# Feed-forward gate and up products: seven block products per feature pair in place of eight, in float32 on one Trainium2 core

## What is computed

```python
D_FF = 2816

def _swiglu(h, w1, w3, w2):
    return (jax.nn.silu(h @ w1) * (h @ w3)) @ w2

def second_block(x, ...):
    ...
        x = x + 0.5 * _swiglu(_rms_norm(x, ffn1_norm[layer]),
                              ffn1_w1[layer], ffn1_w3[layer], ffn1_w2[layer])
        ...
        x = x + mixed @ w_out[layer]
        x = x + 0.5 * _swiglu(_rms_norm(x, ffn2_norm[layer]),
                              ffn2_w1[layer], ffn2_w3[layer], ffn2_w2[layer])
```

## Time and profile before

| | us |
|---|---|
| median of 3 runs (lowest, highest) | 2481.8 (2480.57, 2481.88) |
| span of the profiled execution | 2479.0 |
| TensorE busy | 2412.7 (97%) |
| VectorE busy | 1413.9 (57%) |
| ScalarE busy | 1041.5 (42%) |
| GpSimd busy | 288.2 (12%) |

### The profile page before, as it was taken

The page is one execution under the profiler, slowest core; times in us unless marked ns, Lnnn a source line. Parts: engine busy times, 40 slices in busy tenths (PEclk is TensorE's granted clock), DMA queues, the critical chain, the costliest instruction groups (busy, mean ns, idle before and its releaser), DMA issues.

```text
span 2479.0 us, 30754 instructions
## 1 busy us (share of the span) xinstructions
PE 2412.7 (97%) x12348; PEld 1874.9 (76%) x12348; DVE 1413.9 (57%) x2056; ACT 1041.5 (42%) x1571; POOL 288.2 (12%) x248
## 2 busy tenths in 40 slices
PE   6999999999899999999999999999999999999999
PEld 4877868687777777777666688888888777888887
DVE  3675776768645777555555674344444767543442
ACT  2424433343545456655555562222343555322221
POOL 0010111212232411111111100000122000000000
PEclk9999999999999999999999999999999999999999
DMA  7324234342446369999999722332332112323322
GB/s 278 115 67 171 90 136 132 102 132 83 141 158 228 121 256 400 424 423 423 423 422 423 313 85 86 101 102 78 101 115 71 43 43 68 103 81 107 96 78 81
DMA packets 116083, 427.77 MB, mean 173 GB/s; under 512 B 15977, under 2 KB 30569, under 8 KB 90208
## 3 DMA queue, kind: packets, MB, share of 16 engines
q1 hardware_dynamic: 91488, 377.42, 41.3%
q10 hardware_dynamic: 13440, 25.17, 2.8%
q0 software_dynamic: 11008, 23.16, 2.7%
HBM read 411.08 MB, written 31.72 MB: 179 GB/s over the span
## 4 chain that ended last, share of the span: by engine, by line
PE 77%; DMA 10%; DVE 8%; ACT 4%; issue 1%; SPq 0%; ACTq 0%; POOL 0%; DVEq 0%; POOLq 0%
PE bank L762 19%; PE bank L764 18%; PE bank L763 18%; DMA pair<-in_ed 8%; PE bank L1354 2%; PE bank L1332 1%; PE bank L1334 1%; PE bank L1333 1%; DVE HLB L432 1%; PE bank L1404 1%; DVE HLB L295 1%; ACT HLB L421 1%; PE bank L1713 1%; DMA raw<-in_wxbc 1%; PE bank L1736 1%
## 5 line engine op out<-in xcount | busy, mean ns | idle before, releaser
L432 DVE TENSOR_TENSOR HLB<-raw,HLB 128x1024 fp32r<-128x1024 f32 (+1 forms) x286 | 346.1, 1213 | 369.9 <-ACT HLB L421 369.6
L762 PE MATMUL bank<-HTh,HLB 128*128 128x512 f32 (+1 forms) x1358 | 545.2, 401 | 10.4 <-DVE HLB L432 7.5
L764 PE MATMUL bank<-HTh,HLB 128*128 128x512 f32 (+1 forms) x1358 | 528.8, 389 | 0.0
L763 PE MATMUL bank<-HTl,HLB 128*128 128x512 f32 (+1 forms) x1358 | 524.9, 387 | 0.0
L421 ACT ACTIVATE HLB<-raw 128x1024 fp32r<-128x1024 f32 (+1 forms) x294 | 289.8, 991 | 298.3 <-PE bank L764 270.9
L762 PEld LDWEIGHTS bank<-HTh,HLB 128*128 128x128 f32 x1358 | 257.1, 189 | 90.7 <-issue 27.5
L764 PEld LDWEIGHTS bank<-HTh,HLB 128*128 128x128 f32 x1358 | 256.4, 189 | 57.1
L763 PEld LDWEIGHTS bank<-HTl,HLB 128*128 128x128 f32 x1358 | 257.1, 189 | 53.0 <-issue 1.9
L763 PE MATMUL bank<-FAl,HLB 128*128 128x512 f32 x352 | 138.9, 395 | 0.0
L764 PE MATMUL bank<-FAh,HLB 128*128 128x512 f32 x352 | 138.9, 395 | 0.0
L762 PE MATMUL bank<-FAh,HLB 128*128 128x512 f32 x352 | 138.9, 395 | 0.0
(11 more groups left out here) (632 smaller groups left out, 4432.5 us busy)
## 6 DMA issues: line engine op xcount, KB each, us to landing
raw<-in_f SPq DMA_DIRECT2D x120, 512.0 KB, 3.4
pair<-in_ed SPq DMA_DIRECT2D x32, 1024.0 KB
ht_pair<-in_eu SPq DMA_DIRECT2D x31, 1024.0 KB, 22.5
raw<-in_wada SPq DMA_DIRECT2D x40, 512.0 KB, 4.1
raw<-in_eg SPq DMA_DIRECT2D x17, 1024.0 KB, 7.1
pair<-in_eu SPq DMA_DIRECT2D x17, 1024.0 KB
ht_pair<-in_eg SPq DMA_DIRECT2D x17, 1024.0 KB
ht_pair<-in_ed SPq DMA_DIRECT2D x16, 1024.0 KB, 20.0
```

The lines of the kernel that those rows point to most:

```text
L432: self.nc.vector.tensor_tensor(lo, raw, hi.bitcast(F32), ALU.subtract).then_inc(*self.w_lo.next(n))
L762: mm(bank, ah, bh, start=(start and i == 0), stop=False)
L763: mm(bank, ah, bl, start=False, stop=False)
L764: ins = mm(bank, al, bh, start=False, stop=(stop and i == n - 1))
```

## The change

Of the 11 feature pairs of a network, pair 0 stays as it was. In the ten others w1 and w3 are taken as one matrix. For a pair, the weights form 2 x 2 blocks: rows are the even and the odd feature (each with its 128 columns of w1 and of w3), columns are the input features 0 to 511 and 512 to 1023. A block is again 128 x 1024 and is called r11, r12 (even), r21, r22 (odd). The tokens' matrix is cut the same way: B11, B12 (input features 0 to 511, tokens 0 to 255 and 256 to 511), B21, B22. Instead of eight block products seven are made, after Strassen and Winograd, in the order a11, s1, a12, s3, s2, a22, s4. A block product is 24 matmuls of 256 columns into one bank, w1's result in its first half and w3's in the second.

Four of the seven weight operands are sums. GpSimd makes them in place, with additions of 128 x 1024: s1 = r21 + r22 (into the slot "chain"), s3 = r21 + r11, s2 = s1 + r11, s4 = r12 + s2. Six slots of their own hold the blocks; loads wait until a slot was split or summed. All seven operands then go through the split by ScalarE and VectorE.

Four token operands are sums too: T1 = B11 - B12, T3 = B12 - B22, T2 = B22 + T1, T4 = B21 - T2. They are made once per network: ScalarE writes XT times the gain to BS (eight passes), VectorE makes four sums over 128 x 1024, and these are split (T3 into the place of B12).

Banks per pair: x takes a11, is copied out by ScalarE (SNAP) and then a12 is added to it; z takes s1, is copied (ZSNAP), and s4 is added; w, y, v take s3, s2, a22. VectorE combines them (U2, U3, C22) to the four results, scales the gate's by RN, and, after ScalarE's Silu, multiplies with the unscaled up results. RN's second factor is put in behind the down product: two VectorE operations for each of its results. The down products come after chunks of 3, 3, 3 and 2 pairs (6, 6, 6 and 4 features), so there are 32 results instead of 16, and their tiles are 768 or 512 wide. In a chunk, the gates, copies and remainders of a pair are done during the next one ("behind").

```diff
+CHUNKS = ((0, 1, 2), (3, 4, 5), (6, 7, 8), (9, 10))
...
+BLOCKS = ("r21", "r22", "chain", "r11", "r12")
+BLOCK_OF = {"a11": "r11", "s1": "chain", "a12": "r12", "s3": "r21", "s2": "chain", "a22": "r22", "s4": "r12"}
...
+        had = self.before[(name, p, block)]
+        if had is not None:
+            if had[2] == "r11":
+                engine.wait_ge(*self.summed(*had[:2], "s2"))
+            else:
+                engine.wait_ge(*self.split(*had[:2], {"r21": "s3", "chain": "s2", "r12": "s4", "r22": "a22"}[had[2]]))
+            if had[2] == "chain":
+                engine.wait_ge(*self.summed(*had[:2], "s4"))
...
+        for block, part in (("r21", 2), ("r22", 3), ("r11", 0), ("r12", 1)):
+            self.free(sp, name, p, block)
+            self.nc.sync.dma_start(self.raw(name, p, block), source[p - 1, part]).then_inc(
+                *self.loads[self.place[(name, p, block)]].next((name, p, block)))
...
+    def add(self, name, p, op, a, b):
+        self.nc.gpsimd.tensor_tensor(self.raw(name, p, BLOCK_OF[op]), self.raw(name, p, a), self.raw(name, p, b),
+                                     ALU.add).then_inc(*self.pool_out.next((name, p, op)))
...
+            def block(op, bank, operand, *ready, start=True):
+                xh, xl = operand
...
+                for n in range(8):
+                    out, k = bank[:, half(n // 4)], n % 4
+                    mm(out, w.hi[:, n, :], xh[:, k, :], start=(start and n == 0), stop=False,
+                       skip_group_check=not start)
+                    mm(out, w.hi[:, n, :], xl[:, k, :], start=False, stop=False, skip_group_check=not start)
+                    ins = mm(out, w.lo[:, n, :], xh[:, k, :], start=False, stop=(n == 7), skip_group_check=not start)
+                ins.then_inc(*pe_out.next((q, p, op)))
+                ring.done(w)
...
+            x = psum.take(pe, (q, p, "x"))
+            block("a11", x, B11)
+            z = psum.take(pe, (q, p, "z"))
+            block("s1", z, T1, dve_out.when(("tt", name, 0)))
+            block("a12", x, B21, act_out.when(("s", q, p)), start=False)
+            block("s3", psum.take(pe, (q, p, "w")), T3, dve_out.when(("tt", name, 3)))
+            block("s2", psum.take(pe, (q, p, "y")), T2, dve_out.when(("tt", name, 1)))
...
+            block("a22", psum.take(pe, (q, p, "v")), T4, dve_out.when(("tt", name, 2)))
...
+            block("s4", z, B22, act_out.when(("zs", q, p)), start=False)
...
+            for c in range(3):
+                begun.append(ring.take(pe, w2, c, WIDE * chunk))
+                psum.take(pe, (w2, chunk, c))
+                products(c, begun[c], range(n - 2), stop=False)
+            for c in range(3):
+                ended(c, begun[c], products(c, begun[c], range(n - 2, n), start=False))
...
+                activation(BS[:, k, :], XT[:, k, :], ACT.Copy, scale=C(name, k)).then_inc(*act_out.next(("bs", name, k)))
...
+        def act_pair(name, w2, q, p, behind):
+            first = p == CHUNKS[p // 3][0]
+            act.wait_ge(*pe_out.when((q, p, "a11")))
...
+            activation(SNAP[:, :], psum[(q, p, "x")][:, :], ACT.Copy).then_inc(*act_out.next(("s", q, p)))
+            ring.hi(act, q, p, "a11")
+            if behind:
+                act_gated(name, 2 * p - 1)
+            act.wait_ge(*pe_out.when((q, p, "s1")))
...
+            activation(ZSNAP[:, :], psum[(q, p, "z")][:, :], ACT.Copy).then_inc(*act_out.next(("zs", q, p)))
+            ring.hi(act, q, p, "s1")
+            if behind:
+                act_gated(name, 2 * p - 2)
+            for op in ("a12", "s3", "s2", "a22"):
+                ring.hi(act, q, p, op)
+            act_silu(name, 2 * p + 1)
+            ring.hi(act, q, p, "s4")
+            act_silu(name, 2 * p)
...
+            act_rows(name)
+            for f in range(2):
+                ring.hi(act, w1, f)
+                ring.hi(act, w3, f)
+                if f == 0:
+                    act_rms(name, ("gr", 3) if name == "n2" else None)
+                    for i in range(3):
+                        act_sum(name, i)
+                act_silu(name, f)
+                act_gated(name, f)
+            act.wait_ge(*pe_out.when((w3, 0, 1)))
+            act_sum(name, 3)
...
+            tensor_tensor(s1, s1, s3, ALU.subtract).then_inc(*dve_out.next(("sum", name, 0)))
+            tensor_tensor(s3, s3, s2, ALU.subtract).then_inc(*dve_out.next(("sum", name, 3)))
...
+            tensor_tensor(s2, s2, s1, ALU.add).then_inc(*dve_out.next(("sum", name, 1)))
...
+            tensor_tensor(s4, s4, s2, ALU.subtract).then_inc(*dve_out.next(("sum", name, 2)))
...
+        def dve_gates_odd(name, q, p):
+            dve_gates(name, 2 * p + 1, U3[:, half(1)], C22[:, half(1)])
+
+        def dve_gates_even(name, q, p):
+            dve_gates(name, 2 * p, psum[(q, p, "x")][:, half(1)], U2[:, half(1)])
+
+        def dve_pair(name, q, p, behind):
...
+                dve_gates_odd(name, q, p - 1)
+            ring.lo(dve, q, p, "a11")
+            if behind:
+                dve_gates_even(name, q, p - 1)
+            ring.lo(dve, q, p, "s1")
+            if behind:
+                dve_rest(name, 2 * p - 1)
+                dve_rest(name, 2 * p - 2)
+            dve.wait_ge(*pe_out.when((q, p, "a12")))
...
+            dve_scale(even[:, half(0)], psum[(q, p, "x")][:, half(0)], 0)
+            ring.lo(dve, q, p, "a12")
+            ring.lo(dve, q, p, "s3")
...
+            tensor_tensor(U2[:, :], psum[(q, p, "y")][:, :], SNAP[:, :], ALU.subtract).then_inc(
...
+            tensor_tensor(U3[:, :], psum[(q, p, "w")][:, :], U2[:, :], ALU.add).then_inc(*dve_out.next(("u3", q, p)))
...
+            tensor_tensor(C22[:, :], U3[:, :], ZSNAP[:, :], ALU.subtract).then_inc(*dve_out.next(("c22", q, p)))
+            ring.lo(dve, q, p, "s2")
...
+            dve_scale(odd[:, half(1)], C22[:, half(0)], 1)
...
+            tensor_tensor(U3[:, :], psum[(q, p, "v")][:, :], U3[:, :], ALU.add).then_inc(*dve_out.next(("c21", q, p)))
...
+            dve_scale(odd[:, half(0)], U3[:, half(0)], 0, ("t", name, 2 * p + 1))
+            ring.lo(dve, q, p, "a22")
...
+            tensor_tensor(U2[:, :], psum[(q, p, "z")][:, :], U2[:, :], ALU.subtract).then_inc(
...
+            dve_scale(even[:, half(1)], U2[:, half(0)], 1, ("t", name, 2 * p))
+            ring.lo(dve, q, p, "s4")
...
+            dve_sums(name)
...
+                tensor_tensor(t[:, :], psum[(w1, 0, f)][:, :], RN[:, :], ALU.mult).then_inc(
+                    *dve_out.next(("t", name, f)))
+                if f == 0:
+                    for i in range(3):
+                        dve_sum(name, i)
...
+                tensor_tensor(t[:, :], t[:, :], psum[(w3, 0, f)][:, :], ALU.mult).then_inc(*dve_out.next(("g", name, f)))
+                dve_rest(name, f)
+            dve_sum(name, 3)
...
+                    tensor_tensor(y[:, :], psum[(w2, chunk, c)][:, :], RN[:, :], ALU.mult).then_inc(
+                        *dve_out.next(("r", w2, chunk, c)))
...
+                    scalar_tensor_tensor(out=XT[:, c, :], in0=y[:, :], scalar=0.5, in1=XT[:, c, :],
+                                         op0=ALU.mult, op1=ALU.add).then_inc(*dve_out.next((w2, chunk, c)))
...
+            def first(p):
+                pool.wait_ge(*quads.loaded(name, p, "r21"))
+                pool.wait_ge(*quads.loaded(name, p, "r22"))
+                quads.free(pool, name, p, "chain")
+                quads.add(name, p, "s1", "r21", "r22")
+
+            first(1)
+            for p in range(1, 11):
+                pool.wait_ge(*quads.summed(name, p, "s1"))
+                pool.wait_ge(*quads.loaded(name, p, "r11"))
+                quads.add(name, p, "s3", "r21", "r11")
+                pool.wait_ge(*quads.split(name, p, "s1"))
+                quads.add(name, p, "s2", "chain", "r11")
+                pool.wait_ge(*quads.split(name, p, "a12"))
+                pool.wait_ge(*quads.summed(name, p, "s2"))
+                quads.add(name, p, "s4", "r12", "chain")
+                if p < 10:
+                    first(p + 1)
...
+            sp.wait_ge(*pe_out.when(("yl", 1, 3)))
...
+            sp.wait_ge(*pe_out.when(("wo2", 7)))
```

336 lines of the change are left out of this document (243 added, 93 removed).

## The result

The changed kernel takes 2507.2 us (median of 4 runs, 2506.35 to 2513.64) against 2481.8: 1.0106 times the time before, interval 1.0091 to 1.0121. It is slower by 25 us. The forecast was 2485 with a range of 2448 to 2522, and slower was the likelier sign with 0.44. The time lies in the range, 22 us above the point, in the part that had been given to rival B and to chains longer than forecast. B's mechanism did not occur; a longer chain did, at a place that the prediction had passed over.

What follows compares the result with a forecast made beforehand. TensorE's matmuls were taken to bound the feed-forward stretches. Terms -50.6 + 26 + 18 + 7 + 1.2 + 1.4 = +3 us on a span of 2479.0 gave 2482, with 2.8 for the median 2485 us; range 2448 to 2522.

Steps and rivals of the forecast that it cites:

- slower was the likelier sign: Whole kernel: chance 0.44 of slower, against 0.36 faster and 0.2 same.
- rival B: Chunks: blocks load late, three or four additions fall into the pair; +36 us, 2521; chance 0.27 together with longer chains.
- chains longer than forecast: Whole kernel: dependent work takes longer than put; no size of its own, chance 0.27 together with rival B.
- What bounds the kernel: Both feed-forward stretches: they last as long as TensorE's matmuls, until another engine is late.
- The saving: Twenty pairs on TensorE: 19.4 us a pair instead of 21.96, with 2.78 per block; 50.6 us less (43 to 58).
- The side sum by the isolated gaps: TensorE's matmuls: the saving by the Trainium skill's gap of N/2.4 + 2.5 ns would be 47 us.
- Exclusion of VectorE and GpSimd: Each pair: additions and VectorE work with two SBUF inputs exclude each other; 24.2 us against TensorE's 19.4.
- Waits in the chunks: Third blocks wait for ScalarE's copy: second pair 1 us, third 5.5 us late; 26 us for both networks (18 to 42).
- Start of the networks: First pair's third block late: 18 us in the first network (12 to 22), 7 us in the second (3 to 11).
- The small ones: Last down chunks 1.2 us, an extra VectorE operation per down result at both networks' ends 1.4 us.
- A: Pairs and starts: engines do overlap, or chains are shorter than put; -29 us, 2453; chance 0.22.
- C: Block products: 256-column blocks don't halve, weight loads bound each matmul; 30 us a pair for 22, +160 us; chance 0.01.

Runs made afterwards that it cites:

- e3: The changed kernel with the 80 additions of weight blocks on VectorE, between its splits, instead of GpSimd: 2482.3 us.
- e4: The changed kernel with GpSimd's additions of pairs 2 to 10 cut to 8 of 1024 columns, all waits kept: 2483.1 us in one run.
- e1: The changed kernel with ScalarE's copy of bank x of the next pair ahead of the even feature's Silu in a chunk: 2492.4 us.
- e2: The changed kernel with ScalarE making the next weight's high part before writing and squaring the finished XT row, at the first network's end: 2499.75 us.
- e8: The kernel of e6 with chunks of 2, 3, 3, 3 pairs instead of 3, 3, 3, 2: 2466.9 us.
- e6: The changed kernel with the edits of e1, e2 and e3 together: 2472.0 us.
- e5: The changed kernel with GpSimd's first two additions of the first network held until VectorE has made the first 256 tokens' remainders: 2504.9 us.

## Why the prediction was right and wrong

**What bounds the kernel.** Right. TensorE without waits took 19.84 us a pair wherever the other engines were ahead.

**The saving.** Right in kind, 7 us too large. A block in the middle of a pair takes 2.83 us, which is the upper end of the span of 2.72 to 2.83; the middle had been taken. The side sum by the isolated gaps of the Trainium skill (TensorE: Matmul & The Clock Gate, Back-to-back issue gap) comes to 48 us, not 47. The whole pair in the two stretches of products before came to 22.0 us, as put.

**Exclusion of VectorE and GpSimd.** Right (e3, e4), and an addition lasts 2.52 us on the mean, most of them 2.35 to 2.5, where 2.4 was taken. Averaged over the kernel VectorE lost only 1.4 us for each (e4), but in the chain of a last pair nearly what was charged (below). Bank reads were let through, as assumed: L3523 starts at 1580.15, inside an addition, and takes 0.68 us.

**Waits in the chunks.** The place, the releaser and the cause were right, shown by e1: the third block, ScalarE's copy, the Silu ahead of it. The sum was 19 for 26. The last pairs waited for 3.2 us on the mean, where 5.4 was worked out (49.8 less 44.4) and 5.5 put. The first of them shows the two halves of the error, counted from its chunk's start at 1562.26. The copy ended at 48.9 us, 0.9 earlier than 49.8: six additions took 10.5 us from VectorE's operations (each beside the same one in e4), where 14.4 - 2.1 - 1 = 11.3 had been charged. And TensorE was due at the third block at 45.6, 1.2 later than 44.4, since its blocks take 2.83 us and not 2.78 and the second pair loses 0.3. A part of the shorter wait came back as the low clock behind it (1.6 us in two of four cases), which the forecast did not have. The second pairs lost 0.3 us, not 1.

**Start of the networks.** 18.3 for 18, and 5.8 for 7. For the first one the waits are 4.6 us for the first block's split (4 or 5 were forecast), 9.0 for the copy and 1.1 for T1, together 14.7; of the rest 3.0 is low clock (the first block's 24 matmuls start within 4.35 us instead of 2.71, the third's within 4.13 instead of 2.79). For the second one the wait for the copy is 3.6 us, and the low clock behind it costs 1.6. So a part of the agreement is luck: the waits were shorter, and the clock made it up.

**"The small ones", the step that failed.** The prediction counted the extra VectorE operation per down result once, 0.69 us on the path at the end, and said that the work under the down products stays below their 33.5 us. This was reckoned for chunks of six features and without the mixer's preparation. At the first network's end a chunk has four, so that a product lasts 2.8 us instead of 7.7, and each result also drives a high part, a square, a low part and the next split, in a circle through two engines that takes 5.05 us. It cost 17.5 us where 1.3 stood. e2 and e8 show both halves: the order of ScalarE (9.5 us of this stretch in e2), and the length of the product that covers a result (the other 8.2 from e6 to e8, with which the stretch is as short as before).

**The missing step.** GpSimd's first additions were placed "in the start" but not against what VectorE does in that very moment, ahead of it. They need only loaded blocks and ran as soon as these had landed, in the middle of the remainders that TensorE waited for: 6.3 us with the clock (e5: 4.5 of them back; e3, which has no addition on GpSimd there: 6.0).

**The rivals.** A fell with e3 and e4. B's mechanism did not occur: no wait of TensorE is for a GpSimd sum, and its 2521 was near the result for no reason of its own. C fell with 19.84. That the result lies in the range is luck in part: the upper end was drawn for B, and the two steps that carried the time there, 17.5 and 6.3 us, stood at 1.3 and at nothing.
